# Four moves in a hybrid encoder layer: norm-weight sizes, an SBUF offset, the order of two kinds of transfer, and a late store

## The reference

```python
proj = rms_norm(x, norm_mix) @ w_in            # q | k | v | ssm input | attention gate | ssm gate
q, k = rope(rms_norm(q, q_norm)), rope(rms_norm(k, k_norm))
attn = gqa_attention(q, k, v) @ w_attn_proj    # 16 query heads, 4 key/value heads, head_dim 64
y = gelu(s5_bidirectional(u, ...))             # 32 groups of 16 channels, 64 complex states
ssm = (y @ w_glu_a) * sigmoid(y @ w_glu_b)
x = x + (sigmoid(g_attn) * attn + sigmoid(g_ssm) * ssm) @ w_out
x = x + square(relu(rms_norm(x, norm_mlp) @ w_ff1)) @ w_ff2
```

## Time and profile before

| | |
|---|---|
| median of 3 runs | 2373.91 us (2373.36 to 2374.01) |
| the profiled execution | 2368.7 us, its span 2366.9 us |
| PE busy | 2304.6 us, 97% |
| DVE busy | 1798.7 us, 76% |
| POOL busy | 1342.5 us, 57% |
| ACT busy | 1191.5 us, 50% |
| mean granted PE clock | 0.996 |

### The profile page before, as it was taken

One profiled execution on the slowest core, in us unless ns is written; L12 is line 12 of the kernel. 1 busy time (PEld: TensorE's weight loads), 2 busy tenths in 40 slices (PEclk: granted clock), 3 DMA queues, 4 the chain that ended last, 5 costly groups with the idle time before them and its releaser, 6 DMA issues.

```text
span 2366.9 us, 44111 instructions
## 1 busy us (share of the span) xinstructions
PE 2304.6 (97%) x14871; PEld 2000.9 (85%) x14871; DVE 1798.7 (76%) x2613; ACT 1191.5 (50%) x1980; POOL 1342.5 (57%) x1113
## 2 busy tenths in 40 slices
PE   6999999999988999999999999999999999999999
PEld 5788888888855666678888889999999999999999
DVE  6788577888877777766676778888888977777776
ACT  5556212121176777744434347555556565555563
POOL 0000864564466767744444427677766976666765
PEclk9999999999999999999999999999999999999999
DMA  5233334334334221144666663233333452222222
GB/s 191 93 118 113 120 106 128 111 115 108 111 98 96 53 51 37 35 146 150 204 204 198 205 210 134 92 98 102 98 97 114 147 175 72 72 72 72 72 72 90
DMA packets 186969, 271.02 MB, mean 115 GB/s; under 512 B 50352, under 2 KB 104880, under 8 KB 186672
## 3 DMA queue, kind: packets, MB, share of 16 engines
q1 hardware_dynamic: 186224, 268.63, 37.1%
q10 hardware_dynamic: 576, 0.27, 0.0%
HBM read 201.13 MB, written 57.67 MB: 109 GB/s over the span
## 4 chain that ended last, share of the span: by engine, by line
PE 87%; DMA 5%; DVE 3%; issue 1%; SPq 1%; ACT 1%; POOL 1%; ACTq 0%; DVEq 0%; POOLq 0%
PE banks L65 9%; PE banks L67 9%; PE banks L66 9%; PE banks L3218 6%; PE banks L3220 6%; PE banks L3221 6%; PE banks L3242 6%; PE banks L3244 6%; PE banks L3245 6%; DMA block<-stage 4%; PE p_acc L65 3%; PE p_acc L67 3%; PE p_acc L66 3%; PE banks L2105 2%; PE banks L2106 2%; PE banks L2074 2%
## 5 line engine op out<-in xcount | busy, mean ns | idle before, releaser
L2712 POOL TENSOR_TENSOR t_wlo<-f_sums,t_whi 128x512 fp32r<-128x512 f32 x256 | 360.3, 1410 | 155.5 <-ACT t_whi L2743 155.5
L3000 DVE TENSOR_TENSOR f_x<-banks,f_x 128x384 f32<-128x384 f32 x448 | 245.0, 552 | 94.7 <-PE banks L3245 94.4
L1902 POOL TENSOR_TENSOR a_plo<-a_p 128x512 f16<-128x512 f32 x236 | 248.4, 1059 | 115.5 <-ACT a_p L1948 111.6
L1948 ACT ACTIVATE a_p<-banks,s_scales 128x512 f32<-128x512 f32 x320 | 248.1, 777 | 96.1 <-PE banks L2106 70.8
L2698 POOL TENSOR_TENSOR t_wlo<-t_wraw,t_whi 128x1024 fp32r<-128x1024 f32 x67 | 164.8, 2460 | 225.5 <-ACT t_whi L2728 225.4
L2743 ACT ACTIVATE t_whi<-f_sums 128x512 fp32r<-128x512 f32 x256 | 161.8, 632 | 231.6 <-PE banks L3245 147.3
L3218 PE MATMUL banks<-block,t_whi 128*128 128x384 f32 x720 | 241.6, 336 | 2.4 <-ACT stage L2857 1.6
L3221 PE MATMUL banks<-block,t_wlo 128*128 128x384 f32 x720 | 240.5, 334 | 0.0
L1981 DVE TENSOR_REDUCE stage<-banks 128x1 f16<-128x1024 f32 (+1 forms) x184 | 190.6, 1058 | 60.4 <-PE banks L2074 59.4
L3220 PE MATMUL banks<-block,t_whi 128*128 128x384 f32 x704 | 235.2, 334 | 0.0
L3242 PE MATMUL banks<-block,t_whi 128*128 128x384 f32 x608 | 203.4, 334 | 1.8 <-DVE f_x L3000 1.8
(11 more groups left out here) (428 smaller groups left out, 6837.4 us busy)
## 6 DMA issues: line engine op xcount, KB each, us to landing
t_wraw<-w_tail_t SPq DMA_DIRECT2D x136, 512.0 KB, 4.0
a_quotient<-w_tail_t SPq DMA_DIRECT2D x64, 512.0 KB, 3.8
w_raw<-w_in_t SPq DMA_DIRECT2D x31, 512.0 KB, 3.9
proj_scratch<-s_gate SPq DMA_DIRECT2D x48, 256.0 KB, 2.1
t_graw<-proj_scratch SPq DMA_DIRECT2D x24, 512.0 KB, 3.7
block<-roped_scratch SPq DMA_DIRECT2D x146, 64.0 KB, 2.2
p_sw<-p_qn SPq DMA_DIRECT2D x60, 128.0 KB, 2.1
mix_scratch<-a_quotient SPq DMA_DIRECT2D x48, 128.0 KB, 4.3
```

The source lines that it names most:

```text
L1902: pool.tensor_tensor(p_lo[s][:], p32[s][:], p_hi[s], ALU.subtract).then_inc(plo_pool, 1)
L1948: act.activation(p32[kt % QKP][:], ps[:, ST_BANK + kt % 2], ACT.Exp, bias=mid.p_top, scale=mid.score_scale).then_inc(exp_done, 1)
L2712: pool.tensor_tensor(weights_of(t, ring_lo[t % 4]), source(t), f32(weights_of(t, ring_hi[t % 4])), ALU.subtract).then_inc(lo_pool.sem, 1)
```

## The change

1. `gain_sizes()` is called ahead of the 21 adds of squares, no longer behind 14 of them.
2. `s_d` (128 bytes a partition) is allocated ahead of `x_rs` and the weight buffers, no longer behind them; they all move by 128 bytes, to multiples of 256. What is allocated behind `s_d`'s old place stays.
3. In attention SP waits for and places the maxima of unit u + 2 first, then waits for the scores of u and loads queries.
4. The wait for the last head's output, the load of `ones` and the two stores become `last_store()`, called at the end of round 1 of the tail's first block.

```diff
         sb("s_align", [P, 24])
+        self.dd = sb("s_d", [GC, GROUPS])
         self.rs = sb("x_rs", [P, TOK])
...
-        self.dd = sb("s_d", [GC, GROUPS])
...
+            gain_sizes()
             for b in range(NBLK):
                 for k in range(1, KD):
                     add_square(b, k)
                 if b == 1:
-                    gain_sizes()
                     low(0, 3)
                     scale_gains()
...
                         for kv in range(NKV):
                             u = sq.u0 + it * 4 + kv
+                            if next_seq(sq, last, kv):
+                                place = mid.place_max if next_seq(sq, last, kv) is A else mid.place_max_parts
+                                place(sp, u + 2, (kv + 2) % 4)
                             sp.wait_ge(scored, sq.s0 + sq.n * (it * 4 + kv + 1))
                             if not last_g:
                                 mid.load_q(sp, roped, kv, g + (4 * kv + 1), blk)
                             elif blk + 1 < NBLK:
                                 mid.load_q(sp, roped, kv, 4 * kv, blk + 1)
-                            if next_seq(sq, last, kv):
-                                place = mid.place_max if next_seq(sq, last, kv) is A else mid.place_max_parts
-                                place(sp, u + 2, (kv + 2) % 4)
...
             next_w(0, 1, 1)
-            sp.wait_ge(fore.moved, LAST_PAIR + 2)
-            sp.dma_start(ones[:], ones_d).then_inc(const_in, 16)
-            for half in range(2):
-                sp.dma_start(mix[0:8].rearrange("t p n -> (t p) n").rearrange("(h d) n -> h d n", d=HEAD)
-                             [NQ - 1 - NKV * (1 - half)][:, TOK - BLK:TOK],
-                             fore.o[t_last][half * HEAD:(half + 1) * HEAD]).then_inc(st.attention[t_last], 16)
+
+            def last_store():
+
+                sp.wait_ge(fore.moved, LAST_PAIR + 2)
+                sp.dma_start(ones[:], ones_d).then_inc(const_in, 16)
+                for half in range(2):
+                    sp.dma_start(mix[0:8].rearrange("t p n -> (t p) n").rearrange("(h d) n -> h d n", d=HEAD)
+                                 [NQ - 1 - NKV * (1 - half)][:, TOK - BLK:TOK],
+                                 fore.o[t_last][half * HEAD:(half + 1) * HEAD]).then_inc(st.attention[t_last], 16)
...
                     if m + 2 < KD:
                         sp.wait_ge(sg_ready, b * KD + m + 2)
                         sp.dma_start(g_raw[m % 2][:], gates[m + 2][:, :, blk_of(b)]).then_inc(g_in[m % 2], 16)
+                    if (b, m) == (0, 1):
+                        last_store()
```

## The result

The changed kernel takes 2335.78 us, median of 4 runs (2330.94 to 2341.26), against 2373.64 in the same session: a ratio of 0.9842, 95% interval 0.9819 to 0.9864, or 37.9 us less. Measured again in a later session (5 runs, 2329.99 to 2334.87) it takes 2330.95 against 2373.24: 0.9827 (0.9813 to 0.9840). The forecast was 2327.7, with a range of 2320 to 2342. So it is faster, as forecast, but by some 4 to 8 us less; and its runs spread over 10 us, while those of the kernel before spread over 1 in that first session (over 5 to 8 in the later ones).

A forecast was written before the change was run, and what follows sets the result against it. PE, busy 97% of the span, bounds the kernel, through its waits and its matmul pace. Gains of 12.3 + 12.7 + 15.2 + 6.0 = 46.2 us take 2373.9 to 2327.7, range 2320 to 2342.

The forecast's parts named there:

- Edit 1: Before attention: sizes called ahead of the adds end PE's 10.43 us wait at line 1041; gain 12.3 us, bounds 10.4 to 12.4.
- slow restart: After a long wait PE runs eight matmuls 0.43 us apart instead of 0.23; 1.6 us in the tail.
- Edit 2: Projection and gates: weights at multiples of 256 save 0.14 us a tile over 91 tiles; 12.7 us, bounds 0 to 13.4.
- Edit 4: Start of the tail: weights issued sooner end PE's 4.52 us wait and slow restart; gain 6.0 us, bounds 3 to 6.7.
- Edit 3: Attention: placing maxima ahead of query loads gains 15.2 us as a whole, bounds 6 and 20.
- 17.2 in B: Attention, sequence B: waits for placed maxima go over 30 units; 17.2 us gained, 18.2 at most.
- Sum for A: a loss of 2.0: Attention, sequence A: later queries cost 2.0 us in all, bounds a loss of 8 and a gain of 2.
- 0.2 us a unit: Attention, sequence A: each unit becomes about 0.2 us longer as queries go out later; 14 units, 2.9 us.
- I add 1.2 (half a round of issues): Attention, A's first units: SP waits for late maxima, costing a further 1.2 us.
- give back 2.1: Passage from A to B: four placings in a burst (4.8) become spread ones (2.7), giving back 2.1 us.
- the second rival: Attention, B: queries behind the maxima land late, so the new order gains nothing and costs 2; 2344.9 us, chance 0.06.
- the offset rival: Projection and gates: the weights' start isn't the cause, the projection keeps 5.58 us a tile; 2340.4 us, chance 0.11.

The follow-up runs named there:

- edits 1 and 4 alone: Kernel before with only the earlier sizes call and the later last store: 2353.64 us, ratio 0.9921.
- address experiments: Changed kernel with some weight buffers off multiples of 256, one execution each: w_raw off 2332.13 us, w_lo off 2337.26, w_hi off 2343.84, all at 192 2340.59.
- edit 3 undone: Changed kernel with queries again loaded ahead of the placing of maxima, the other three edits kept: 2340.75 us, ratio 0.9868.
- edit 2 alone: Kernel before with only s_d moved, so x_rs and the weight buffers start at multiples of 256 bytes: 2362.5 us, ratio 0.9955.
- the new order in B alone: Changed kernel with maxima placed first only in sequence B's rounds, queries first in A's: 2326.93 us, ratio 0.9808.
- second profile: Changed kernel, unchanged, profiled and timed again in a later session: median 2330.95 us, ratio 0.9827.
- the orders that leave A's first units alone: Changed kernel with maxima first only from unit 8 on (2325.05 us, ratio 0.9802) or only in B's rounds (2326.93 us, ratio 0.9808).

## Why the prediction was right, and where it was off

- **Edit 1** (12.3 us): right. The wait and the slow restart went, the small new wait is 0.38 us and not 0.2. With edits 1 and 4 alone the third sum comes 12.25 us sooner and attention 11.7.
- **Edit 2** (12.7): right in cause, slightly large. The address experiments show the cause. The pace fell from 232.5 to 227.2 ns, 24 x 5.3 = 0.127 us a tile and not the 0.14 that two stretches gave, so 91 x 0.127 = 11.6; alone it brought attention 10.4 forward and the time 10.7 down.
- **Edit 4** (6.0): right. The rest of the span is 6.6 us shorter in the first profile, 6.4 in the second, 5.8 with edits 1 and 4 alone, 8.0 with edit 3 undone; it differs by 0.6 between the kernel before and edit 2 alone, which share the tail. The slow restart here was somewhat longer than the eight matmuls taken from edit 1's: those from 1047.03 to 1050.87 stood 0.43 apart before.
- **Edit 3** (15.2): here the sum failed. "17.2 in B" held: B's first 30 units, 267.76 before, take 251.34 with the new order in B alone and 250.99 in the changed kernel's second profile, 16.4 and 16.8 less. "Sum for A: a loss of 2.0" did not. From unit 0 to unit 16 the second profile has 91.7 us, where edit 3 undone has 84.7: 6.9 lost. Its 0.2 us a unit is right where SP's list is full (units 9 to 14: 1.4 to 1.6 us measured, 1.2 by that rate). The term that was mis-sized most is the one for the first units, "I add 1.2 (half a round of issues)": units 0 to 8 lost 5.9 us against edit 3 undone, where the prediction had 9 x 0.2 + 1.2 = 3.0. About 1 us of the 5.9 is the lower granted clock, for which the prediction had no term in attention. I took SP's wait for late maxima as a small delay of queries; but there the queries' issues were made inside that wait, so the new order adds the whole wait to them, 3.8 us in the round shown (637.27 against 633.46). The second mis-sized term is the passage, which was to "give back 2.1": unit 15 is 0.5 us shorter (7.99 against 8.54). The loss was within the bounds given for A (a loss of 8). The mechanism is that of the second rival, in A and in one round of B: there the queries behind the placings take 5.3 to 7.7 us to land, and PE waits 1.2 to 3.9 us for them in six of the ten profiled executions with the new order in B.
- **The rest of the gap** is chance that the forecast had no term for: a transfer that lands 8 to 10.5 us after its issue, at the passage, and the clock that falls with the wait for it. In the first profile units 15 to 19 took 50.49 us, in the second 42.94. Only profiled executions show it, so how many of the others have it is not known; that the second session's five lie 5 us lower, four of them within 1 us, fits with it.

Term by term, for the second profile (span 2328.2, 38.7 below before's): 23.0 until attention (25.0 forecast), 9.3 in attention to unit 46 (15.2), 6.4 in the rest (6.0).

How near the forecast came is in part luck. By its own bounds the four edits gave 2320 to 2335; the first session's 2335.78 lies outside that, and inside 2320 to 2342 only because the range had been widened for the offset rival, which the address experiments refute. The forecast also carried over the 5.2 us by which before's median lay above its profiled execution. In the changed kernel's second session that distance is 1.0 us, so the forecast is 3.3 us off by the medians and 7.5 by the spans. Ratios near the forecast's (2327.7 to 2373.9, 0.9805) were measured for the orders that leave A's first units alone: 0.9802 and 0.9808.

What stays open: why transfers land late at the passage in two of the thirteen profiled executions of changed kernels, one with the new order and one with the old (edit 2 alone), and why the queries of unit 18's round do in three. That the two 512 KB loads of the tail's weights crowd the passage is neither shown nor excluded: both late landings come with these loads ahead, but so do nine profiles without one, and only two profiles have the loads moved. Whether fewer small packets would help was not tried.

## What to carry to other kernels

When two kinds of transfer share one list, put first the one that is ready first, in each stage by itself: what stands behind a wait loses the whole wait, and here the order that gains 16 us in B loses 7 in A. Before trusting a rate from a steady stretch, look at the stage's first units, where the waits in the list are longest. Before comparing two stretches, look at the granted clock of both. And where float32r matmuls of 128x512, each with its own weight load, run back to back, let the weight buffers start at a multiple of 256 bytes, as here; the distance between matmul starts shows what it gives, the durations don't.

## What the runs showed of the hardware that I had not expected

- A weight tile's start sets the pace of float32r matmuls of 128x512: 227.2 ns at a multiple of 256, 232.5 to 233.4 at 128 past it, 229.0 at 192, though a weight load's record lasts 188 to 191 ns at either start. The Trainium skill, "TensorE: Matmul & The Clock Gate", in "Step-by-step: what each phase is for", has the next weights load behind the running matmul. These runs agree that it does, at every start: a load of 188 ns fits in the 227 to 233 ns between two matmul starts. That the load is then free they don't bear out at 128 past a multiple of 256, where a matmul takes 5 to 6 ns more. And one tensor off the grid slows the matmul ahead of it too.
- A single transfer can land far later than its like. At the passage from A to B a placing landed 10.5 us and a query load 9.5 us after issue in the changed kernel's first profile, where the second has 5.8 and 4.1 at the same places. The profile of edit 2 alone has 10.0 for a placing and 8.0 to 8.4 for two query loads.
- A wait of PE is dearer than its length when the clock falls in it: behind the 7.57 us at the passage unit 16 took 11.31 us at a mean granted clock of 0.74, and 8.52 at 1.00 in the other profile.
